# Turned keys of the sample group's differential attention copied out of PSUM by ScalarE and VectorE in turn

## The reference

```python
def diff_core(q, k, v, qpos, kpos, bias_b, lam, lam_init, subln_g):
    logits = jnp.einsum('bqhcd,bkhcd->bhcqk', q, k) * (B_HEAD_DIM ** -0.5) + bias
    p = jax.nn.softmax(jnp.where(causal, logits, -jnp.inf), axis=-1)
    w = p[:, :, 0] - lam * p[:, :, 1]
    o = jnp.einsum('bhqk,bkhe->bqhe', w, v)
    return rmsnorm(o, subln_g) * (1.0 - lam_init)

def diff_sample(qb, kb, vb, cache_k, cache_v, page_table, ...):
    k_all = concatenate([gather_pages(cache_k, page_table), kb], axis=1)   # 4096 cached + 4 new keys
    v_all = concatenate([gather_pages(cache_v, page_table), vb], axis=1)
    return diff_core(qb, k_all, v_all, past + arange(t), arange(past + t), ...)
```

## Time and profile before

| what | value |
|---|---|
| time, median of 3 runs | 2789.16 us (2782.91 to 2795.84) |
| profiled execution, its own time | 2793.66 us |
| its span | 2791.8 us |
| mean granted TensorE clock | 0.952 of full speed |
| busy time TensorE / VectorE / ScalarE / GpSimd | 2468.1 / 1070.6 / 658.9 / 508.5 us |
| B chunks of the sample group | about 673 to 1100 us of the span |

### The profile page before, as it was taken

One profiled execution on the slowest core, in us unless ns is written; L12 is line 12 of the kernel. 1 busy time (PEld: TensorE's weight loads), 2 busy tenths in 40 slices (PEclk: granted clock), 3 DMA queues, 4 the chain that ended last, 5 costly groups with the idle time before them and its releaser, 6 DMA issues. The chain is left out here.

```text
span 2791.8 us, 31616 instructions
## 1 busy us (share of the span) xinstructions
PE 2468.1 (88%) x12301; PEld 1541.9 (55%) x12321; DVE 1070.6 (38%) x2316; ACT 658.9 (24%) x1627; POOL 508.5 (18%) x622
## 2 busy tenths in 40 slices
PE   7999988867787887788797975999999999989999
PEld 4644435644454554456343452456666666668888
DVE  4579988831565666434131140311212112110000
ACT  2321114545453444344010141110101011100000
POOL 1120221123564554565000100000000000000000
PEclk9999998988998999899898998999999999999999
DMA  3212001035997987555302004021111111021100
GB/s 127 71 58 72 25 3 36 1 111 200 337 335 243 331 297 247 143 172 140 137 1 105 0 1 147 4 59 35 38 38 38 38 33 36 23 92 56 55 16 14
DMA packets 145343, 273.03 MB, mean 98 GB/s; under 512 B 13905, under 2 KB 81674, under 8 KB 145162
## 3 DMA queue, kind: packets, MB, share of 16 engines
q0 software_dynamic: 49408, 176.19, 18.7%
q1 hardware_dynamic: 94588, 90.50, 9.8%
q10 hardware_dynamic: 1200, 4.33, 0.4%
HBM read 257.23 MB, written 13.61 MB: 97 GB/s over the span
## 5 line engine op out<-in xcount | busy, mean ns | idle before, releaser
L595 PE MATMUL PS<-X,XT 128*128 128x512 f32 (+5 forms) x864 | 330.6, 538 | 4.1 <-DMA X<-w_in 4.1
L2578 PE MATMUL PS<-XT,ffn_wg 128*128 128x352 f32 x1056 | 322.6, 463 | 0.9 <-DMA ffn_wg<-w_gate 0.9
L2588 PE MATMUL PS<-XT,ffn_wu 128*128 128x352 f32 x1056 | 316.0, 459 | 0.0
L2588 PEld LDWEIGHTS PS<-XT,ffn_wu 128*128 128x128 f32 x1056 | 200.6, 190 | 111.8
L2578 PEld LDWEIGHTS PS<-XT,ffn_wg 128*128 128x128 f32 x1056 | 198.2, 191 | 109.5 <-issue 6.0
L595 PEld LDWEIGHTS PS<-X,XT 128*128 128x128 f32 (+1 forms) x864 | 154.4, 183 | 166.4 <-issue 140.7
L1797 ACT COPY X<-PS 128x512 f32<-128x512 f32 x352 | 194.1, 592 | 218.6 <-PE PS L1678 131.3
L839 DVE TENSOR_SCALAR_CACHE_REDUCE mask<-score,cand 128x384 bf16<-128x384 f32 (+2 forms) x198 | 181.5, 942 | 3.2
L2067 PE MATMUL PS<-dn_w,H 128*128 128x256 f32 x704 | 155.2, 383 | 8.6 <-DMA dn_w<-w_down 8.6
L2067 PE MATMUL PS<-XT,H 128*128 128x256 f32 x704 | 153.3, 380 | 0.0
L2067 PEld LDWEIGHTS PS<-dn_w,H 128*128 128x128 f32 x704 | 134.6, 192 | 29.2 <-DMA dn_w<-w_down 9.1
(11 more groups left out here) (376 smaller groups left out, 3478.0 us busy)
## 6 DMA issues: line engine op xcount, KB each, us to landing
ffn_wg<-w_gate SPq DMA_DIRECT2D x22, 512.0 KB, 3.6
ffn_wu<-w_up SPq DMA_DIRECT2D x22, 512.0 KB, 3.7
X<-w_in SPq DMA_DIRECT2D x4, 2048.0 KB, 7.8
XT<-w_down SPq DMA_DIRECT2D x2, 2816.0 KB, 13.9
X<-x_prompt ACTq DMA_DIRECT2D x8, 512.0 KB, 7.3
wo_w<-w_out SPq DMA_DIRECT2D x4, 1024.0 KB, 9.5
X<-x_prompt SPq DMA_DIRECT2D x8, 512.0 KB, 12.7
ms_keys<-cache_mem_k SPq DMA_DIRECT2D x8, 512.0 KB, 5.1
```

The costliest lines, as they stand in the source:

```text
L595: last = nc.tensor.matmul(M.PS[0:n, s % 3, 0:chunks[j].width], XT[:, c, t * P:t * P + n], w[:, j % 2, c, 0:chunks[j].width], start=(c == 0 ...
L2578: last = nc.tensor.matmul(M.PS[:, G0 + x, 0:TW], wg[:, f % 2, c, :], XT[:, c, x * TW:(x + 1) * TW], start=(c == 0), stop=(c == KC - 1))
L2588: last = nc.tensor.matmul(M.PS[:, U0 + x, 0:TW], wu[:, f % 2, c, :], XT[:, c, x * TW:(x + 1) * TW], start=(c == 0), stop=(c == KC - 1))
```

## The change

The one counter `t_read` becomes two, one for each bank, and a fill x waits with `wait_read` for the copy of fill x-2 by the count of its own bank. Of the two fills of a kind-B "k" step, ScalarE copies the first (x = 0) as before; VectorE, in its own "k" step, copies the second. Kind A, the indexer and the probabilities stay with ScalarE. The waits before index scores and logits are for both banks.

```diff
+    t_read = [S.sem(f"t_read{x}") for x in range(2)]
...
+    def wait_read(eng, x):
+
+        eng.wait_ge(t_read[x % 2], x // 2 + 1)
+
     def pe(eng):
         def bank(key):
             x = fill[key]
             if x >= 2:
-                eng.wait_ge(t_read, x - 1)
+                wait_read(eng, x - 2)
             return M.PS[:, T0 + x % 2, :]
...
-            eng.wait_ge(t_read, fill["i", h, g, a4, 3] + 1)
+            for x in range(2):
+                wait_read(eng, fill["i", h, g, a4, 3] - x)
...
             if not walk.new(n):
-                eng.wait_ge(t_read, fill["k", n, 3, 1 if kind == "B" else 0] + 1)
+                for x in range(2):
+                    wait_read(eng, fill["k", n, 3, 1 if kind == "B" else 0] - x)
...
-            eng.wait_ge(t_read, fill["p", n] + 1)
+            wait_read(eng, fill["p", n])
...
         def turned(key, dst):
             x = fill[key]
             eng.wait_ge(t_full, x + 1)
-            nc.scalar.copy(dst, M.PS[0:dst.shape[0], T0 + x % 2, 0:dst.shape[1]]).then_inc(t_read, 1)
+            nc.scalar.copy(dst, M.PS[0:dst.shape[0], T0 + x % 2, 0:dst.shape[1]]).then_inc(t_read[x % 2], 1)
...
             elif step[0] == "k":
                 n = step[1]
-                for key in walk.fills(step):
+                for key in walk.fills(step)[0:1]:
                     j, x = key[2:]
                     turned(key, kt[:, j, x * CH:(x + 1) * CH])
...
                 topk = cuts()
+            elif step[0] == "k":
+                for key in walk.fills(step)[1:2]:
+                    x = fill[key]
+                    eng.wait_ge(t_full, x + 1)
+                    nc.vector.tensor_copy(kt[:, step[2], CH:2 * CH], M.PS[:, T0 + x % 2, :]).then_inc(t_read[x % 2], 1)
             elif step[0] == "s":
```

More of the change, by code:

```diff
@@ L1540, in keys_at @@
         return kv[:, j, h * 512:], loaded[h][j]
-    (t_full, t_read, i_done, relu_done, sc_mm, sc_done, w_mm, w_ready, s_done, st_done, d_done, p_ready, a_ready,
+    t_read = [S.sem(f"t_read{x}") for x in range(2)]
+    (t_full, i_done, relu_done, sc_mm, sc_done, w_mm, w_ready, s_done, st_done, d_done, p_ready, a_ready,
      pv_done, o_done, om_ready, om_mm, mixed, chain, cand_ready, cand_moved, cut_ready, cut_moved, mask_ready,
      o_ss, o_ms, o_rs) = (S.sem(n) for n in (
-         "t_full", "t_read", "i_done", "relu_done", "sc_mm", "sc_done", "w_mm", "w_ready", "s_done", "st_done",
+         "t_full", "i_done", "relu_done", "sc_mm", "sc_done", "w_mm", "w_ready", "s_done", "st_done",
          "d_done", "p_ready", "a_ready", "pv_done", "o_done", "om_ready", "om_mm", "mixed", "chain", "cand_ready",
```

## The result

| | before | after |
|---|---|---|
| time, median (4 runs each) | 2791.74 us | 2893.35 us (2884.12 to 2900.16) |
| ratio, 95% interval | | 1.0362 (1.034 to 1.0384) |
| profiled execution, its span | 2791.8 us | 2882.3 us |
| mean granted TensorE clock | 0.952 | 0.935 |

The change costs some 100 us. The forecast was 2870 us, 2820 to 2925. The profiled execution of the changed kernel is the fastest of its four (2884.12 us), so what the profiles show, 90.5 us, is less than the 101.6 between the medians.

The account below looks back on a forecast made before the run. No engine is full; a loop of waits through VectorE's queue bounds the B chunks. Queue 77, less 9 swallowed by waits for values, plus 13 for the clock: +81 on 2789.2, so 2870 us, range 2820 to 2925.

Parts of the forecast that it names:

- The bound: B chunks: ScalarE has slack; a loop of waits through VectorE's queue sets the next chunk's start, 3.44 us after outputs.
- The hand-stepped chunks: Chunks 12, 10 and 26, stepped with measured durations: outputs later by 3.6, 1.7 and 2.4 us, mean 2.57.
- The queue's term: VectorE's first key copy stands behind a search round: 30 chunks x 2.57 = 77 us, less 9 swallowed by waits for values.
- the clock's: TensorE's matmuls slow after standing still: half of 16 chunks lose 1.66 us, +13 us, with ends 0 and 50.
- a period of up to 12.9: Loop of gathering a chunk's values after the outputs before it: at most 12.9 us, against a measured period of 12.05.
- The waits for VectorE: Sign: TensorE's key transposes wait for VectorE 2 to 3.5 us in each of 30 chunks, next to nil before.
- The period of B chunks: Sign: time from one B chunk to the next near 16 us after the change.
- DMA share: Sign: DMA engines' busy share of the B stage falls from 0.86 to about 0.72.
- Relief wins: Rival: both engines empty banks side by side, half of TensorE's 39.8 us of waits for ScalarE goes: 2769 us; chance 0.03.
- The transfers hide it: Rival: transfers and the values' loop set the period, a third of the shift shows: +26, 2815 us; chance 0.10.
- The clock falls in every chunk: Rival: TensorE's gaps lower its clock in each chunk, term 50 or more: +118, 2907 us; chance 0.15.
- What delays the outputs delays the next chunk by as much: B chunks: the next chunk starts 3.44 us after this one's outputs end, set by VectorE's queue.

Follow-up runs that it names:

- Experiments 2: Changed kernel with VectorE copying only the second half of a chunk's first key step: 2901.11 us, ratio 1.0386; only of its last: 2791.23 us, 0.9994.
- experiment 3: Changed kernel with the top-k search round moved from the s to the p step: 2799.58 us, ratio 1.0023; same move in the kernel before: 2784.25 us.
- the run with the gap filled: Changed kernel with 16 unread transposes between the halves of key step j = 1 in 29 B chunks: 2859.62 us, ratio 1.0231.
- the split kernel: Kernel before with VectorE copying the second of each two B key fills, that is the changed kernel: 2893.35 us, ratio 1.0362.
- experiment 7: s round moved to p, o round ahead of the outputs wait: changed kernel 0.9961, repeated 0.9969; kernel before 1.0003; that with last copy on VectorE 0.9988.
- Experiment 6: Kernel before with the o step's search round moved ahead of the wait for outputs: 2790.13 us, ratio 0.9987.

## Why the prediction held, and where it was short

**The bound.** That ScalarE's copies were not what the kernel waits for, and that a round in VectorE's queue stands between the reduce and the first key copy, was right to the row: predicted 4.18 us from the reduce to the second half (836.86 less 832.68), measured 4.11. Experiments 2 and 3 show it, from two sides: one copy for each chunk behind the round costs all, one next to the outputs nothing, and with the round moved the loss is 6 us.

**The hand-stepped chunks.** For chunk 12 I forecast that outputs start 3.6 us later. In the changed kernel it is 4.8, and in the run with the gap filled, which has VectorE's queue but not the lower clock, 3.6 (10.29 for 6.69), and the chunk lasts 15.66 us where the prediction had 12.05 + 3.6 = 15.65. So chunk 12 was stepped rightly but for the clock. The other two fit less well. In chunk 10 outputs start 9.49 us after the reduce (849.84 less 840.35), where my steps give 8.23; in chunk 26 it is 11.03 (1103.59 less 1092.56) for 10.68, and 9.74 with the gap filled. In chunk 10 the clock is at 0.89 in both runs, and I had stepped it at full speed. That the mean of three chunks carried over to thirty is partly luck.

**The queue's term.** 2.57 less 0.3, thus 2.27 us for each chunk and 68 in all. In the run with the gap filled the 30 chunks are 68.2 us longer than in the kernel before, 2.27 each, and the whole kernel 64.5 us (2.31% of 2792), with a little of the filler's cost in both, and of the clock's. The waits for values were swallowed as forecast: from eight to one. One reading in it was loose: "11.0 us at most" and "a period of up to 12.9" were worked out from the median of the landing, 6.0 us; with the longest, 7.5, it is 14.4.

**The term that was too small is the clock's.** I took +13 of at most 50: half of 16 chunks losing 1.66 us. The filler gives back 37 us, its own cost included. The step that failed is "I let half of these lose 1.66", and in it the count, 8 chunks: the clock falls in 29 of the 30. The price for each was about right: the filler gives the clock back in 18 chunks (29 less 11), and 37 / 18 is 2.1 us each. But it does not fall where I had it: in chunk 12 V takes 0.67 us more and the transposes 0.84, in the keys and not in the outputs. The Trainium skill, TensorE: Matmul & The Clock Gate, Part 1, has the array halved after idling; the rows of chunk 12 agree (0.57 behind a gap of 3.39 us). My doubt, that the trace did not show such a gap in each chunk, cost the forecast 37 - 13 = 24 us. That is about all of the 23 between 2870 and 2893. By the profiles the term is smaller: the stage is 26.6 us shorter with the filler (522.1 for 548.7), 1.5 us for each of the 18, but they show the changed kernel at its fastest and the filled one at its slowest.

**What I said it would show.** The waits for VectorE: 99 us in the view, forecast 60 to 105, but in 41 waits and not 30. The period of B chunks: 15.8 and 16.7 us, forecast near 16. DMA share: 0.77 over 502 us, forecast 0.72 over 508.

**The rivals.** *Relief wins* did not come, though its first half did: waits for ScalarE before key transposes fell by 22 us. I had put its point of decision at a round of under 0.5 us; with no round ahead of the first three copies of a chunk (experiment 3) the split kernel is still 0.2% over before, so that point was too kind: there the relief does not outweigh VectorE's own lateness. With the o step's round moved as well (experiment 7) the split kernel is 0.3 to 0.4% ahead of before, though only where the kernel before takes some 2915 us. *The transfers hide it*: no, the DMA share fell. *The clock falls in every chunk* is what happened, in 29 of 30, though I gave it 0.15; its time, 2907, is 14 us over the 2893 measured, mine 23 under. The number fell into the range, and the better account of the clock was the rival's.

**What I took the loops to be.** "What delays the outputs delays the next chunk by as much" holds for delays: 4.79 and 4.80 us in chunk 12. Experiment 6 shows that it does not hold for gains: the loop of the values is right behind.

What stays open: how the 37 us divide between TensorE's matmuls and what the filler costs; why half a round less gives back 61 us and the second half only 34; what the unnamed waits in the runs of experiment 7 are; and whether its gain holds without them.

## What to carry to other kernels

Before a copy goes to a less busy engine, look at what stands ahead of it in that engine's program order, and not at the engine's busy share: VectorE was at 61% (260 of 427) and still 3 us late each time, because work without a deadline, the search's rounds, stood ahead of work that another engine waits for. Put such work where the engine would wait anyway, behind the copies. And price a new gap on TensorE twice: once as the gap, and once for the slower matmuls behind it.

## What the runs showed of the hardware

464 transposes that nobody reads made the kernel 37 us faster (29 to 45), by holding the granted clock of the stage at 0.94 in place of 0.86. After a gap of 3.39 us, twelve matmuls of 128x128 took 1.55 us for 0.88, and eight transposes 1.92 for 1.08; the same twelve after a gap of 1.65 us, behind the 16 added transposes, ran at full speed (0.88). In the changed kernel the granted clock was below 1.00 in 29 of 30 chunks, whose waits for a copy were 2.15 to 5.06 us, and not in the one where it was 1.79. That is no limit: in chunk 26 of the kernel before, the outputs ran at the lower level after 1.11 us.
